# Two transformer-like blocks on one core: delta rule's products by chunk, masks for the SSM decays, a last block by halves, and first k-tiles one slab ahead

## The chip, the cores and the metric

The kernel is one program on one core of a Trainium2 chip. The metric is device time in microseconds (us) of one execution. PE is TensorE, PEld its weight loads, ACT ScalarE, DVE VectorE, POOL GpSimd, SP the queue engine that issues most DMAs.

## What is computed

All arrays are float32: 256 tokens, width 2048. The first block is a norm and a projection to an SSM (32 heads of 64, 4 groups, chunks of 128 tokens) and to windowed attention with sinks, their output projection, a gated feed-forward of width 5632 with a short convolution, and an embedding (`pe`) that is normalised and added through a gate:

```python
gate = jax.nn.sigmoid(_rmsnorm(h, ple_norm_g[i]) @ w_ple_gate[i])
pe = _rmsnorm(p[i] @ w_ple_proj[i], ple_post_g[i])
h = h + gate * pe
```

The second block has a gated delta rule in both directions (8 heads of 128, chunks of 64 tokens), a Fourier branch, gates, an output projection, an MLP of width 8192 with squared relu, and the last norm. Of the delta rule, each chunk needs the inverse of a unit lower triangular 64x64 matrix:

```python
kb = k * beta
m = jnp.where(strict, jnp.einsum("bhnid,bhnjd->bhnij", kb, k) * decay, 0.0)
a_mat = m + jnp.eye(CHUNK, dtype=m.dtype)
rhs = jnp.concatenate([v * beta, kb * jnp.exp(gc)[..., None]], axis=-1)
sol = lax.linalg.triangular_solve(a_mat, rhs, left_side=True, lower=True, unit_diagonal=True)
```

In the SSM, the decay between tokens s and l of a chunk is the exponential of the sum of `dt * a` over the tokens after s up to l.

## The kernel before, in words

**The weight stream.** All large weights come as 238 quads of 4 slabs. A slab is 128 x 1024 float32: two k-tiles by 512 columns. For each slab SP loads `w_raw` (after DVE's `lo_ready` of the slab in the same place), ACT casts it to `w_hi` (after PE's `slab_done` of the slab before in that place), DVE subtracts to get `w_lo`. PE then makes 12 matmuls of 512 columns: two k-tiles, two token tiles `t` of 128, and three products (high by high, high by low, low by high), as `slab` writes them, into the pair of banks `psum[t]`. A `chunk` is 8 slabs, a product of full depth 2048 by 512 columns. Each engine's order is written out by hand in its own block, and semaphores tie them. `split` is the name of the cast on ACT and of the subtraction on DVE.

**The activations** (`a_hi`, `a_lo`) are made per tile of two k-tiles: PE transposes four squares of h (`operand_tiles`, line 2078), ACT scales and rounds to `a_hi` (`gained`, line 752), DVE makes `a_lo` (`gained_rest`, line 1297). The first chunk of the program is `first_chunk`: it transposes four tiles, and then tile s+4 ahead of slab s.

**SSM groups.** In each of four groups and for both token tiles, PE makes rows of summed decays from `adt` broadcast and a triangle `before` (line 2216), DVE subtracts each head's own sum and clips at 0 (line 1522, eight instructions), ACT takes the exponential of `ssm_w`, POOL multiplies by the scores (line 611), and PE applies it (`within`, line 2228). POOL also roots, scales and rotates q and k in `qk_norm`, between these products. `qk_square` shares memory with `ssm_y`.

**End of the first feed-forward and the gates.** PE makes the embedding (line 2378), then the last down projection and with it the transposes for the gate product. DVE does `normalize(pe_tok, ...)` (line 1322) in one piece before it adds the down products to h (line 1361). The gate product is four chunks, each with a sigmoid and a multiplication by `pe_tok`.

**Delta rule.** Four turns, two heads each. A unit is a token tile by a direction, 128 x 128, with two chunks on its diagonal. The triangular inverse is made in levels 1 to 5 (level 0 by a mask): `level_z` (line 2469), ACT's copy to `zz` (line 1156), `level_rz` (line 2477), DVE's update (line 1827), transposes `turned` (line 2487) and DVE's copy. POOL masks for the next level (line 686) and makes scaled copies of q, k and v, the query's at level 1 (line 694). Half slabs of the gates' weight stream (`gate_slab`) stand between these products on PE. After the levels come `uw` (2564, 2565) and four steps of the state, whose products are 64 wide (`of_state` line 2502, `output_of_state` line 2495), and for which forward and backward direction write different halves of the partitions.

**The last block.** The MLP runs in 16 blocks of 512 hidden columns: an up chunk, transposes of `m_stage` (line 2146), relu (1243), square (1246) and gating (1993), `m_lo` (1999), then `mlp_down` of two quads. The last one is followed by the squares of h, the mean, POOL's root, the scaling and four output transfers (line 518).

## Time and profile before

| | |
|---|---|
| median of the runs | 3024.98 us (3024.2 to 3029.27, 3 runs) |
| the profiled execution | 3025.64 us, of which the span 3023.8 us |
| PE, PEld, DVE, ACT, POOL busy | 98%, 81%, 67%, 47%, 10% |
| DMA | 525.71 MB, mean 174 GB/s |
| mean granted clock of PE | 0.996 |

Times in the profile count from the span's start. Busy shares are of the span; a matmul's records overlap with the next one's, so the distance between starts, not their length, is what each costs. PEclk is the granted clock: 1.00 is 2.4 GHz, 0.50 is 1.2 GHz.

### The profile page before, as it was taken

Reading aid. Unit: us, or ns where it says so; the run is one execution under the profiler, and the core shown is the slowest. Engines: PE = TensorE matmul, PEld = TensorE weight load, DVE = VectorE, ACT = ScalarE, POOL = GpSimd, SP = SyncE. Lnnn points to the kernel's source line nnn. Section 1 sums busy time; section 2 is a strip of 40 time slices with the busy share of each in tenths; the row PEclk is TensorE's granted clock in tenths of the full one; section 3 lists DMA queues with packets and bytes.
Section 4 is the critical chain, followed back from the end, with each engine's and each line's share of the span. In section 5 each row is a group of like instructions: output and inputs, shape, how many; then the busy total and the mean of one; then the engine's idle time right before and its main releaser. Section 6 shows DMA issues by size and latency. Waiting matters only on the chain.

```text
span 3023.8 us, 42408 instructions
## 1 busy us (share of the span) xinstructions
PE 2973.5 (98%) x14487; PEld 2455.1 (81%) x14487; DVE 2015.8 (67%) x2667; ACT 1410.5 (47%) x1797; POOL 314.3 (10%) x275
## 2 busy tenths in 40 slices
PE   8999999999999999999999999999999999999997
PEld 7888777788888888886878888888888888888886
DVE  6765877656677776667577667776655666666665
ACT  6444446544444444445555543333545444444443
POOL 0003860000000000000000154333000000000000
PEclk9999999999999999999999999999999999999999
DMA  6554443466555555553565433332765565555554
GB/s 221 178 186 159 140 147 132 156 196 210 182 189 178 194 188 194 187 188 125 188 214 187 166 119 112 112 118 96 240 219 195 186 192 189 186 191 188 188 182 135
DMA packets 145653, 525.71 MB, mean 174 GB/s; under 512 B 16416, under 2 KB 17184, under 8 KB 144800
## 3 DMA queue, kind: packets, MB, share of 16 engines
q1 hardware_dynamic: 140416, 504.25, 51.0%
q0 software_dynamic: 1536, 11.78, 1.1%
q10 hardware_dynamic: 3616, 8.52, 0.9%
q8 instruction: 57, 0.93, 0.1%
q14 instruction: 28, 0.23, 0.0%
HBM read 516.09 MB, written 8.39 MB: 173 GB/s over the span
## 4 chain that ended last, share of the span: by engine, by line
PE 65%; issue 25%; DVE 4%; POOL 3%; ACT 1%; DMA 1%; DVEq 0%; ACTq 0%; POOLq 0%; SPq 0%
PE bank L2053 19%; PE bank L2055 19%; PE bank L2054 19%; DVE w_lo L1283 1%; PE bank L2146 1%; PE bank L2477 1%; PE bank L2469 1%; PE bank L2078 1%; ACT w_hi L727 1%; POOL qk_rs L563 1%; DMA w_raw<-weights 0%; PE bank L2284 0%; PE bank L2487 0%; POOL delta L694 0%; POOL delta L686 0%
## 5 line engine op out<-in xcount | busy, mean ns | idle before, releaser
L1283 DVE TENSOR_TENSOR w_lo<-w_raw,w_hi 128x1024 fp32r<-128x1024 f32 x952 | 1193.9, 1264 | 789.6 <-ACT w_hi L727 788.7
L727 ACT CAST w_hi<-w_raw 128x1024 fp32r<-128x1024 f32 x952 | 1000.0, 1052 | 1410.7 <-PE bank L2055 1386.7
L2053 PE MATMUL bank<-w_hi,a_hi 128*128 128x512 f32 x2816 | 1118.9, 397 | 2.1 <-DVE w_lo L1283 1.7
L2055 PE MATMUL bank<-w_hi,a_lo 128*128 128x512 f32 x2816 | 1098.6, 390 | 0.0
L2054 PE MATMUL bank<-w_lo,a_hi 128*128 128x512 f32 x2816 | 1097.6, 390 | 0.0
L2053 PEld LDWEIGHTS bank<-w_hi,a_hi 128*128 128x128 f32 x2816 | 529.8, 188 | 115.9 <-issue 9.5
L2055 PEld LDWEIGHTS bank<-w_hi,a_lo 128*128 128x128 f32 x2816 | 529.2, 188 | 112.2
L2054 PEld LDWEIGHTS bank<-w_lo,a_hi 128*128 128x128 f32 x2816 | 530.0, 188 | 106.3 <-issue 1.9
L539 POOL TENSOR_TENSOR rstd<-rstd,neg_half 128x2 f32<-128x2 f32 x7 | 5.5, 787 | 1927.1 <-DVE rstd L1312 1927.1
L2053 PE MATMUL bank<-w_hi,m_hi 128*128 128x512 f32 x512 | 200.1, 391 | 5.1 <-DVE m_lo L1999 5.1
L2055 PE MATMUL bank<-w_hi,m_lo 128*128 128x512 f32 x512 | 200.0, 391 | 0.0
L2054 PE MATMUL bank<-w_lo,m_hi 128*128 128x512 f32 x512 | 199.9, 390 | 0.0
L1361 DVE TENSOR_TENSOR h<-h,bank 128x512 f32<-128x512 f32 x240 | 153.6, 681 | 22.2 <-PE bank L2055 22.2
L2053 PE MATMUL bank<-w_hi,f_hi 128*128 128x512 f32 x352 | 139.8, 397 | 0.0
L2055 PE MATMUL bank<-w_hi,f_lo 128*128 128x512 f32 x352 | 138.1, 392 | 0.0
L2054 PE MATMUL bank<-w_lo,f_hi 128*128 128x512 f32 x352 | 137.9, 392 | 0.0
L2053 PEld LDWEIGHTS bank<-w_hi,m_hi 128*128 128x128 f32 x512 | 96.6, 189 | 25.5 <-DVE m_lo L1999 5.4
L2054 PEld LDWEIGHTS bank<-w_lo,m_hi 128*128 128x128 f32 x512 | 96.6, 189 | 20.1
L2055 PEld LDWEIGHTS bank<-w_hi,m_lo 128*128 128x128 f32 x512 | 96.5, 189 | 20.1
L2055 PEld LDWEIGHTS bank<-w_hi,f_lo 128*128 128x128 f32 x352 | 66.6, 189 | 14.1
L2054 PEld LDWEIGHTS bank<-w_lo,f_hi 128*128 128x128 f32 x352 | 66.7, 190 | 13.8 <-issue 0.2
L2053 PEld LDWEIGHTS bank<-w_hi,f_hi 128*128 128x128 f32 x352 | 66.7, 189 | 13.6 <-DVE f_lo L1669 0.2
(383 smaller groups left out, 2488.9 us busy)
## 6 DMA issues: line engine op xcount, KB each, us to landing
w_raw<-weights SPq DMA_DIRECT2D x952, 512.0 KB, 4.2
gate<-gate_st ACTq DMA_DIRECT2D x8, 512.0 KB, 3.3
h<-gate ACTq DMA_DIRECT2D x8, 512.0 KB, 5.2
gain<-gains POOLq DMA_DIRECT2D x3, 1024.0 KB, 7.2
h<-x_tok SPq DMA_DIRECT2D x4, 512.0 KB, 9.9
w_proj_sb<-w_proj POOLq DMA_DIRECT2D x1, 2048.0 KB, 10.0
h_rest<-h POOLq DMA_DIRECT2D x1, 2048.0 KB, 13.3
h<-h_rest POOLq DMA_DIRECT2D x1, 2048.0 KB, 10.1
```

The lines of the kernel that those rows point to most:

```text
L539: nc.gpsimd.tensor_tensor(rstd[:, n], rstd[:, n], neg_half[:, 0:TT], ALU.pow).then_inc(rstd_ready, 1)
L563: nc.gpsimd.tensor_tensor(rs, rs, neg_half[:, 0:TT * heads8].rearrange("p (t a) -> p t a", t=TT), ALU.pow).then_inc(qk_rstd, 1)
L727: nc.scalar.copy(w_hi[:, s, :], w_raw[:, s, :]).then_inc(hi_ready, 1)
L1283: V.tensor_tensor(w_lo[:, s, :], w_raw[:, s, :], w_hi[:, s, :].bitcast(F32), ALU.subtract).then_inc(lo_ready, 1)
L1361: V.tensor_tensor(h[:, t, col], h[:, t, col], pair[p][t][:], ALU.add).then_inc(pair_free[p], 1)
L2053: T.matmul(psum[t][:], left_hi[:, ts], wh, start=first, stop=False)
L2054: T.matmul(psum[t][:], left_hi[:, ts], wl, start=False, stop=False)
L2055: last = T.matmul(psum[t][:], left_lo[:, ts], wh, start=False, stop=final)
L2078: last = T.transpose(bank[4 + i % 4][:, k * SEQ + t * P:k * SEQ + (t + 1) * P], src[:, t, (2 * i + k) * P:(2 * i + k + 1) * P], ident[:])
L2146: last = T.transpose(bank[first + ct // 2][:, (ct % 2) * SEQ + t * P:(ct % 2) * SEQ + (t + 1) * P], src[:, t, col0 + ct * P:col0 + (ct + 1 ...
L2469: last = T.matmul(hd.at(2, n), hd.mk[:, t, d], hd.r[:, t, d], start=True, stop=True)
L2477: last = T.matmul(hd.at(2, n), hd.t[:, t, d], hd.zz[:, t, d], start=True, stop=True)
```

## The change

It has these parts.

1. `slab`: all products with the high part of the weights first (after `hi_ready`), then those with the low part (after `lo_ready`). The count is the same.
2. `first_chunk` and ACT's and DVE's beginning: two tiles are transposed first, then tile s+1 ahead of slab s; ACT and DVE make tile s+1 before they split slab s. SP loads in another order.
3. SSM decays: DVE writes `ssm_later`, a mask times `adt`, PE multiplies it by `before`, ACT takes the exponential from the banks. POOL's `qk_norm` becomes `qk_scaled` and `qk_rotated`, and the rotation of tile 0 comes after the second product with the scores. `qk_square(0)` moves to the memory of `bT`.
4. The embedding is scaled per chunk in the gates.
5. Delta rule: the scores and both products of each level are made by chunk (`by_chunk`: two products of 64 x 64 in place of one of 128 x 128); the query's scaling on POOL comes at level 5; slab 8 is halved, with one half ahead of `uw`; DVE's order of splits and updates shifts.
6. The last block: gating and `m_lo` by halves and before DVE's last split; the last two column chunks by token tile; sum, mean, root, scaling and output by token tile.

```diff
@@ sync
-            for c in range(DC):
+            def piece(c):
                 cols = slice(c * NC, (c + 1) * NC)
                 sp_.dma_start(h[:, :, cols], small["x_tok"][:, :, cols]).then_inc(piece_loaded[c], 16)
-                sp_.dma_start(w_raw[:, c, :], wstream[0, c]).then_inc(raw_loaded[c], 16)
+            def first_slab(s):
+                sp_.dma_start(w_raw[:, s, :], wstream[0, s]).then_inc(raw_loaded[s], 16)
+            piece(0)
+            first_slab(0)
+            first_slab(1)
+            piece(1)
+            first_slab(2)
+            first_slab(3)
+            piece(2)
+            piece(3)
@@ gpsimd, SSM group
                     if t == 0:
                         qk_root(g)
-                    qk_norm(g, t)
+                        qk_scaled(g, 0)
+                qk_rotated(g, 0)
+                qk_scaled(g, 1)
+                qk_rotated(g, 1)
@@ gpsimd, delta rule: in the loop over levels k
                             nc.gpsimd.tensor_tensor(hd.eT, hd.eT, cums, ALU.mult).then_inc(dn_eTm, 1)
-                            pool.wait_ge(dn_egb, hd.of(i))
-                            q_rows = hd.qk[:, 0].rearrange("p (t s) -> p t s", t=TT).unsqueeze(2).to_broadcast(shape)
-                            nc.gpsimd.tensor_tensor(hd.qd, hd.qd, q_rows, ALU.mult).then_inc(dn_qd, 1)
...
+                        else:
+                            pool.wait_ge(dn_egb, hd.of(i))
+                            q_rows = hd.qk[:, 0].rearrange("p (t s) -> p t s", t=TT).unsqueeze(2).to_broadcast(shape)
+                            nc.gpsimd.tensor_tensor(hd.qd, hd.qd, q_rows, ALU.mult).then_inc(dn_qd, 1)
@@ scalar, beginning (DVE's has the same order)
+            gained(TR_ATTN, C_ATTN, 0)
             for s in range(QUAD):
-                gained(TR_ATTN, C_ATTN, s)
+                gained(TR_ATTN, C_ATTN, s + 1)
                 split(0, s, s + 1, first=True)
-            for s in range(2):
-                gained(TR_ATTN, C_ATTN, QUAD + s)
+            for s in range(QUAD - 1):
+                gained(TR_ATTN, C_ATTN, QUAD + s + 1)
                 split(Q_XBC + 1, s, s + 1)
-            gained(TR_ATTN, C_ATTN, 6)
-            gained(TR_ATTN, C_ATTN, 7)
-            split(Q_XBC + 1, 2, QUAD)
+            split(Q_XBC + 1, QUAD - 1, QUAD)
@@ scalar, SSM group
                 def decays(t):
-                    act.wait_ge(seg_ready, TT * g + t + 1)
-                    nc.scalar.activation(ssm_w, ssm_w, ACT.Exp).then_inc(seg_exp, 1)
+                    n = TT * g + t
+                    act.wait_ge(row_mm, n + 1)
+                    if n:
+                        act.wait_ge(ydiag_mm, n)
+                    for b in range(2):
+                        last = nc.scalar.activation(ssm_w[:, 4 * b:4 * b + 4].rearrange("p a s -> p (a s)"), bank[4 + b][:], ACT.Exp)
+                    last.then_inc(seg_exp, 1)
@@ vector, SSM
+            def later_tokens(n):
+                g, t = divmod(n, TT)
+                shape = [P, HPG, P]
+                if n:
+                    dve.wait_ge(row_mm, n)
+                V.scalar_tensor_tensor(ssm_later, before[:].unsqueeze(1).to_broadcast(shape), 0.0,
+                                       adt[:, t, g * HPG:(g + 1) * HPG].unsqueeze(2).to_broadcast(shape), ALU.is_equal, ALU.mult).then_inc(seg_ready, 1)
@@ vector, end of the first feed-forward, and per chunk of the gates
-            normalize(pe_tok, pe_tok, N_POST, G_POST)
+            mean_square(N_POST)
...
+                normalized_piece(pe_tok, n, N_POST)
                 for t in range(TT):
                     dve.wait_ge(sig_ready, TT * n + t + 1)
+                    dve.wait_ge(normed, NORMED[G_POST - 1] + TT * n + t + 1)
@@ vector, the last block
+            j = N_FF2 - 1
+            for b in range(2):
+                half = slice(2 * b, 2 * b + 2)
+                dve.wait_ge(ff_silu, N_FF + 2 * j + b + 1)
+                V.tensor_tensor(m_act[:, half].rearrange("p k s -> p (k s)"), m_relu[:, half].rearrange("p k s -> p (k s)"),
+                                bank[6 + b][:], ALU.mult).then_inc(ff_mul, 1)
+                dve.wait_ge(ff_mul, N_FF + 2 * j + b + 1)
+                dve.wait_ge(ff_hi, N_FF + 2 * j + b + 1)
+                V.tensor_tensor(m_lo[:, half], m_act[:, half], m_hi[:, half].bitcast(F32), ALU.subtract).then_inc(ff_lo, 1)
+            mlp_down(N_QUADS - 4, range(D // NC - 1, D // NC))
@@ tensor, slab
+                pe.wait_ge(hi_ready, QUAD * q + s + 1)
+                for j in part:
+                    wh = w_hi[:, s, j * NC:(j + 1) * NC]
+                    for t in range(TT):
+                        for n, left in enumerate(products[j]):
+                            T.matmul(psum[t][:], left[:, t * P:(t + 1) * P], wh, start=start and j == 0 and n == 0, stop=False)
                 pe.wait_ge(lo_ready, QUAD * q + s + 1)
                 for j in part:
-                    left_hi, left_lo = products[j]
-                    wh = w_hi[:, s, j * NC:(j + 1) * NC]
                     wl = w_lo[:, s, j * NC:(j + 1) * NC]
                     for t in range(TT):
-                        ts = slice(t * P, (t + 1) * P)
-                        first = start and j == 0
-                        final = stop and j == SLAB_KT - 1
-                        T.matmul(psum[t][:], left_hi[:, ts], wh, start=first, stop=False)
-                        T.matmul(psum[t][:], left_hi[:, ts], wl, start=False, stop=False)
-                        last = T.matmul(psum[t][:], left_lo[:, ts], wh, start=False, stop=final)
+                        last = T.matmul(psum[t][:], products[j][0][:, t * P:(t + 1) * P], wl, start=False, stop=stop and j == SLAB_KT - 1)
@@ tensor, first_chunk
-                for i in range(4):
+                for i in range(2):
                     operand_tiles(n, src, ready, i)
                 def tiles_of(s):
-                    if s + 4 < KT // 2:
-                        operand_tiles(n, src, ready, s + 4)
+                    if 0 < s < KT // 2 - 1:
+                        operand_tiles(n, src, ready, s + 1)
                     pe.wait_ge(a_lo_ready, KT // 2 * n + s + 1)
@@ tensor, SSM group
-                        last = T.matmul(bank[4 + a // 4][:, (a % 4) * P:(a % 4 + 1) * P],
-                                        adt[:, t, g * HPG + a:g * HPG + a + 1].to_broadcast([P, P]), before[:], start=True, stop=True)
+                        last = T.matmul(bank[4 + a // 4][:, (a % 4) * P:(a % 4 + 1) * P], ssm_later[:, a], before[:], start=True, stop=True)
@@ tensor, delta rule
+                chunks = [slice(c * CHUNK, (c + 1) * CHUNK) for c in range(P // CHUNK)]
+                def by_chunk(out, left, right):
+                    for r in chunks:
+                        last = T.matmul(out[r, r], left[:, r], right[:, r], start=True, stop=True)
+                    return last
...
-                            last = T.matmul(hd.at(2, n), hd.mk[:, t, d], hd.r[:, t, d], start=True, stop=True)
+                            last = by_chunk(hd.at(2, n), hd.mk[:, t, d], hd.r[:, t, d])
...
-                            last = T.matmul(hd.at(2, n), hd.t[:, t, d], hd.zz[:, t, d], start=True, stop=True)
+                            last = by_chunk(hd.at(2, n), hd.t[:, t, d], hd.zz[:, t, d])
```

## Rows read from the trace of the kernel before

**Rows 1.** Who waited for whom, PE: total us, times, longest.

```profile
PE bank L2053 <- DVE m_lo L1999: 5.1, 1, 5.1
PE bank L2228 <- POOL work L611: 3.7, 4, 1.8
PE bank L2078 <- DVE h L1361: 3.5, 1, 3.5
...
PE bank L2469 <- POOL delta L686: 2.1, 4, 0.5
PE bank L2053 <- DVE w_lo L1283: 1.7, 1, 1.7
```

**Rows 2.** Windows: stretch, length, busy us of PE, PEld, DVE, ACT, POOL, PEclk.

```profile
1401.30:1408.10 6.80, 6.08 (x17) 4.82 (x18) 3.90 (x6) 3.11 (x7) 0.00 (x0) 0.50 0.59 177
322.60:326.10 3.50, 3.50 (x17) 3.31 (x16) 2.89 (x5) 0.00 (x0) 3.42 (x2) 0.51 0.78 267
```

**Rows 3.** Timeline, PE, its last matmuls: start us, length, instruction.

```profile
3010.83 0.39 PE L2053 MATMUL bank<-w_hi,m_hi 128*128 128x512 f32 x1
...
3011.28 0.39 PE L2055 MATMUL bank<-w_hi,m_lo 128*128 128x512 f32 x1
```

**Rows 4.** Groups of instructions, PE: one product of the levels; busy, mean ns.

```profile
L2477 PE MATMUL bank<-delta 128*128 128x128 f32 x320 | 39.1, 275 | 0.0
```

**Rows 5.** Timeline, PE: a block of one level, second turn.

```profile
1872.18 0.39 PE L2055 MATMUL bank<-w_hi,a_lo 128*128 128x512 f32 x1
1872.42 1.95 PE L2477 MATMUL bank<-delta 128*128 128x128 f32 x16
...
1874.43 0.40 PE L2054 MATMUL bank<-w_lo,a_hi 128*128 128x512 f32 x1
```

**Rows 6.** Timeline, PE: a block of the state, 64 wide.

```profile
1910.43 0.39 PE L2055 MATMUL bank<-w_hi,a_lo 128*128 128x512 f32 x1
1910.75 0.66 PE L2502 MATMUL bank<-delta 128*64 128x128 f32 x8
1911.23 0.61 PE L2495 MATMUL bank<-delta 128*64 128x128 f32 x8
...
1912.11 0.40 PE L2054 MATMUL bank<-w_lo,a_hi 128*128 128x512 f32 x1
```

**Rows 7.** Timeline, PE: an SSM block of 64 columns.

```profile
300.08 1.97 PE L2228 MATMUL bank<-work 128*128 128x64 f32 x16
```

**Rows 8.** Timeline: ACT and PE between level 5's products.

```profile
1891.97 0.59 ACT L1156 COPY delta<-bank 128x512 f32<-128x512 f32 x1 [0.71 <-PE bank L2469]
1892.66 2.00 PE L2477 MATMUL bank<-delta 128*128 128x128 f32 x16
```

**Rows 9.** Timeline: PE and ACT in the first chunk.

```profile
10.29 1.04 ACT L727 CAST w_hi<-w_raw 128x1024 fp32r<-128x1024 f32 x1 [1.54 <-DMA w_raw<-weights]
...
14.87 0.78 PE L2053 MATMUL bank<-w_hi,a_hi 128*128 128x512 f32 x1
...
25.96 0.60 PE L2078 MATMUL bank<-ident_sb,h 128*128 128x128 f32 x4
...
26.32 0.48 PE L2053 MATMUL bank<-w_hi,a_hi 128*128 128x512 f32 x1
26.60 0.84 ACT L752 ACTIVATE a_hi<-bank,gain_col_sb 128x256 fp32r<-128x256 f32 x2 [1.30 <-PE bank L2078]
...
27.33 1.05 ACT L727 CAST w_hi<-w_raw 128x1024 fp32r<-128x1024 f32 x1
```

**Rows 10.** Timeline, DVE: the embedding's scaling.

```profile
1394.24 5.39 DVE L1322 SCALAR_TENSOR_TENSOR pe_tok<-pe_tok,rstd,gain 128x512 f32<-128x512 f32 x8 [0.83 <-POOL rstd L539]
```

**Rows 11.** Timeline: the last block and the output.

```profile
2983.64 1.15 ACT L1246 ACTIVATE m_hi<-m_relu 128x512 fp32r<-128x512 f32 x2
...
2986.34 1.28 DVE L1999 TENSOR_TENSOR m_lo<-m_act,m_hi 128x512 fp32r<-128x512 f32 x2
...
3016.41 3.21 SPq L518 DMA_DIRECT2D out<-xn_m  x4
```

More of the change, by code:

```diff
@@ L1999, in mlp_gated, with mlp_down @@
                     V.tensor_tensor(m_lo[:, half], m_act[:, half], m_hi[:, half].bitcast(F32), ALU.subtract).then_inc(ff_lo, 1)
[L2001 to L2010 removed]
+            def mlp_down(q, chunks=range(D // NC)):
+                for n in chunks:
+                    split(q + 1 + n // 2, 2 * (n % 2), 2 * (n % 2) + 2)
                     dve.wait_ge(slab_done, QUAD * q + 2 * (n + 1))
@@ L2017, in _, with mlp_up @@
             mlp_evac(q, 0)
-            with dve.Fori(0, N_FF2 - 1) as j:
+            def mlp_up(j):
                 q = Q_MLP + 2 + 4 * j
@@ L2023, in _ @@
                 mlp_evac(q, 2)
-                mlp_down(q + 2, 2)
-            mlp_gated(N_FF2 - 1)
-            mlp_down(N_QUADS - 2, 1, last=True)
-            mean_square(N_OUT)
-            root_of(N_OUT)
+            with dve.Fori(0, N_FF2 - 2) as j:
+                mlp_up(j)
+                mlp_down(Q_MLP + 4 + 4 * j)
+            mlp_up(N_FF2 - 2)
+            mlp_down(N_QUADS - 4, range(D // NC - 1))
+            j = N_FF2 - 1
+            for b in range(2):
+                half = slice(2 * b, 2 * b + 2)
+                dve.wait_ge(ff_silu, N_FF + 2 * j + b + 1)
[4 more added lines that the diff above has]
+                V.tensor_tensor(m_lo[:, half], m_act[:, half], m_hi[:, half].bitcast(F32), ALU.subtract).then_inc(ff_lo, 1)
@@ new lines, in _ @@
+            dve.wait_ge(gain_loaded, 16 * (G_OUT + 1))
+            for n in range(2):
+                split(N_QUADS - 1, 2 * n, 2 * n + 2)
+                dve.wait_ge(slab_done, QUAD * (N_QUADS - 2) + 2 * (n + 1))
+                add_to_h(n, slice(n * NC, (n + 1) * NC))
+                for t in range(TT):
+                    out_gain(t, n)
+            for t in range(TT):
+                for n in range(2, DC):
+                    dve.wait_ge(slab_done, QUAD * (N_QUADS - 1 + t) + 2 * (n - 1))
+                    col = slice(n * NC, (n + 1) * NC)
+                    V.tensor_tensor(h[:, t, col], h[:, t, col], pair[n % 2][t][:], ALU.add).then_inc(pair_free[n % 2], 1)
+                    if n == 2:
+                        out_gain(t, n)
+                end_mean_square(t)
+                if t == 0:
+                    out_gain(t, DC - 1)
@@ L2540, in _ @@
                         for t in range(TT):
-                            ts = slice(t * P, (t + 1) * P)
-                            last = T.matmul(hd.at(1, TT * (1 - a) + t), hd.qk[:, 1, ts], hd.qk[:, a, ts], start=True, stop=True)
+                            for r in chunks:
+                                ts = slice(t * P + r.start, t * P + r.stop)
+                                last = T.matmul(hd.at(1, TT * (1 - a) + t)[r, r], hd.qk[:, 1, ts], hd.qk[:, a, ts], start=True, stop=True)
                     last.then_inc(dn_kk, 1)
@@ L2566, in _ @@
                     last.then_inc(dn_uw, 1)
-                for n in range(8, 11):
+                gate_slab(8, [1])
+                for n in range(9, 11):
                     gate_slab(n)
@@ L2664, in _ @@
                 mlp_block(j)
-            pe.wait_ge(ff_lo, N_FF + 2 * N_FF2)
-            mlp_down(N_QUADS - 2, U_MLP + 2 * (N_FF2 - 1))
+            use = U_MLP + 2 * (N_FF2 - 1)
+            for n in range(2):
+                pe.wait_ge(pair_free[n], 2 * (use + 2 - n))
+                for s in range(2):
+                    pe.wait_ge(ff_lo, N_FF + 2 * (N_FF2 - 1) + s + 1)
+                    slab(N_QUADS - 2, 2 * n + s, [(m_hi[:, 2 * s + k], m_lo[:, 2 * s + k]) for k in range(SLAB_KT)],
+                         pair[n], s == 0, s == 1)
+            for t in range(TT):
+                ts = slice(t * P, (t + 1) * P)
+                for n in range(2, DC):
+                    pe.wait_ge(pair_free[n % 2], 2 * (use + 3 - n % 2))
+                    for i in range(2 * n - QUAD, 2 * n - QUAD + 2):
+                        pe.wait_ge(lo_ready, QUAD * (N_QUADS - 1) + i + 1)
+                        for k in range(SLAB_KT):
+                            tile = 2 * (i % 2) + k
+                            wh, wl = (x[:, i, k * NC:(k + 1) * NC] for x in (w_hi, w_lo))
+                            T.matmul(pair[n % 2][t][:], m_hi[:, tile, ts], wh, start=tile == 0, stop=False)
+                            T.matmul(pair[n % 2][t][:], m_lo[:, tile, ts], wh, start=False, stop=False)
+                            last = T.matmul(pair[n % 2][t][:], m_hi[:, tile, ts], wl, start=False, stop=tile == 3)
+                        last.then_inc(slab_done, 1)
 def _slabs(w, k_major=False):
```

157 lines of the change are left out of this document (89 added, 68 removed).

## The prediction

> **What bounds the kernel now.** I read the page first: TensorE (PE) is busy 98% of the span (the table), and the matmuls of the weight stream follow each other without a hole: from the first of the two rows to the second are two steps in 0.45 us, 0.225 to 0.227 each, so a slab of 12 takes 2.72 us [rows 3]. So only two things are worth time: work that PE does, and the few places where it stands still. The list of PE's waits has the second [rows 1]: 5.1 us before the last MLP block (m_lo), 3.7 us in the SSM groups (work, from POOL), 3.5 us at the end of the first feed-forward (h, from DVE), 2.1 us in the delta rule (delta, from POOL), 1.7 us for one late w_lo. Two of these stops were followed by a stretch at the lower clock: the windows show 3.5 us at 0.51 and 6.8 us at 0.50, that is 1.2 instead of 2.4 GHz [rows 2].
>
> **Delta rule by chunk.** The products of the levels are 128x128 by 128 columns. The group of one of the two lines has 320 instructions [rows 4]; 5 levels, 8 products and 4 turns are 160, so each product is two instructions. Now each product becomes four: 64 wide, 64 columns. A block of 16 with a 128-wide stationary costs, from the last slab matmul before it to the second after it, 1874.43 - 1872.18 = 2.25 us [rows 5]. 16 instructions 64 wide, still 128 columns, cost 1912.11 - 1910.43 = 1.68 us [rows 6]: 8 lie in 0.61 us, one lasts 0.28 [rows 4], so 0.33 us hold the three steps of four pairs, 0.11 a pair, against 0.111 for a single one 128 wide (1.95 less 0.28, over 15, [rows 5]). Two halves of the array work side by side. The fixed part of such a block is 1.68 - 8 x 0.109 = 0.81 us, against 2.25 - 16 x 0.111 = 0.47: entering and leaving the narrow form costs 0.34. The new block has 16 pairs with half the columns, which no row shows. If the columns set the pair, it takes 0.055; if instructions do not start faster than in rows 6, 0.109. For the second speaks nothing but that it is the least seen; for the first, that a full-width instruction takes the same 0.11 with 128 columns, and that 64 columns did not help where the stationary stayed 128 wide (16 in 1.97 us, [rows 7]): there the load of 128 columns sets the pace, and here that load is halved too. I take 0.062, near the first. Block: 16 x 0.062 + 0.81 = 1.80, that is -0.45 us; ends -0.57 and +0.30. Per turn there are 8 such blocks in the levels and one of scores (kk): -4.05. The last level's two products are one block of 32: 32 x 0.062 + 0.81 = 2.79 against 4.02, -1.23; but between them stands ACT's copy, which even now ends at 1892.56 for a start at 1892.66 [rows 8]. With the first product of a head halved the second waits: two copies in a row, 1.18 us, and about 0.3 to reach each side; +0.7. So -4.6 a turn, -18.3 in four. The other levels keep half a slab between their products, 1.36 us, which covers a copy of 0.59. The query decay moves behind level 5, and POOL's 2.1 us [rows 1] go. Half a slab more between the products costs another entry, 0.24 x 4 = +1. Sum -19.4 (ends -25 and +11).
>
> The rows say that the change of form costs 0.34 us a block. The Trainium skill ("TensorEngine Tiling (Array Packing)", Tiling Modes) says that changing the tiling mode drains TensorE, which speaks against mixing narrow blocks with full-width slabs as here. It gives no figure; without any drain the new block would be 1.46 us and the delta rule would save 13 us more, and the measured row decides.
>
> **The start.** This one goes the other way. Before, ACT makes a_hi of tile s, then the cast of slab s, and PE transposes four tiles ahead: tile to slab 0.36 us [rows 9]. After, ACT makes a_hi of tile s+1 before the cast of slab s, and PE transposes tile s+1 only after slab s-1. So slab s can't start before transposes, ACT's a_hi and ACT's cast are through: 0.64 (25.96 to 26.60) + 0.84 + 1.05 + 0.05 = 2.58 us after the first transpose instead of 0.36 [rows 9], 2.2 us for each of the slabs 1 to 6: +13.3. ACT is in order, so the cast cannot pass; that the high part comes first does not help, since it is the high part that is late. On the credit side slab 0 starts when its cast ends, 11.3 instead of 14.87 [rows 9], 3.5 us earlier, but three tiles of 0.36 are then still to do: -2.5. After the cast of slab 6 ACT has one more (1.05), eight squares of h, each about the 0.6 of rows 11, and a narrow cast, which DVE has to split before PE's narrow product: 1.05 + 4.9 + 1.2 = 7.15, against 5.44 for PE's slabs 6 and 7: +1.7. Sum +12.5, ends +10 and +19; the long end is where the stops keep the clock low. I take +13.
>
> **SSM decays.** DVE's pass between PE's rows and ACT's exponential goes (ACT reads PSUM), and POOL multiplies before it rotates; DVE's mask is made a step ahead. The 3.7 us [rows 1] go, with half of the 3.5 us at the lower clock [rows 2]: -5.4 (ends -3 and -6). PE's work is the same count. Late next is the SSM norm, which DVE bounds; unchanged.
>
> **Embedding at the gates.** DVE's scaling, 5.39 us in one piece [rows 10], stood ahead of the add to h that PE waited for. It goes into the gate chunks of 22 us, 1.35 us each, eight slabs long, where DVE has a third of its time idle (the table): nothing. The 3.5 us go, and half of PE's 6.08 busy us at the lower clock [rows 2]: -6.5 (ends -5, -7).
>
> **High part first.** A slab waits for ACT's cast, no longer for DVE's 1.2 us. In the steady stream both are there: nothing. At the late weight (1.7 us, [rows 1]): -1.2 (0 to -2). The order of the matmuls keeps count and loads.
>
> **The end.** The last m_lo comes half by half, ahead of DVE's split and add. From the start of the squares, 2983.64, half a square (0.58) and half a lo (0.64) lead to about 2984.8 [rows 11] instead of PE's start 2.9 us later (5.1 us wait, [rows 1]). Then the output of the first token tile is scaled and sent while PE works on the second: after PE's end at 3011.7 [rows 3] the old tail is 12.1 us, four transfers of 512 KB from 3016.41 on [rows 11]; half of them go (-3.5), and the shorter row of adds, squares and scalings gives about as much as the new order behind ACT (a wait of 1.3) and one of 0.9 for pair 1 take: net -6.3 (ends -4, -8.5).
>
> **Sum.** +13 - 5.4 - 6.5 - 1.2 - 19.4 - 6.3 = -25.8 us on the profiled execution's 3025.64: 2999.8. The median of the runs is 0.7 lower: 2999.
>
> **Rivals.** 1: narrow instructions start no faster than in rows 6, the pair stays at 0.109. Every block costs 0.3 more; +10.6 instead of -19.4: 3029. The Trainium skill ("TensorE: Matmul & The Clock Gate") gives some 62 ns a matmul for the sequencer with hardware decode off; the 0.055 of rows 6 is already under that, so the trace disagrees. Chance 0.15.
> 2, the slower one: in each product the narrow instructions do not pair, since its two passes over one half follow each other, and each takes the 0.11 of rows 7. Then a product costs 0.44 instead of 0.22: 352 products, +77 and the entries: about 3100. It decides (slower by 0.2%) from a mean of 0.056 an instruction on. Rows 6 pair with the same order of halves, against it. Chance 0.03.
> 3: the start does not stall, because ACT's chain is hidden in some way that I miss; -2 instead of +13: 2984. Against it stand two engines in order. Chance 0.12.
> 4: the stops of 2.2 us at the start, or those left in the last block, keep the clock low as the stop in rows 2 did, so that three to five slabs more take twice their 2.72 us: about 3009. Chance 0.12.
> The forecast has 0.58; its own range is 2992 to 3005.
>
> **Numbers.** 2982 to 3022 takes in the forecast, rivals 3 and 4 and the middle of rival 1's pitches. 0.2%, 6 us, is what this kernel's measurement can tell: faster 0.81, same 0.12, slower 0.07.
>
> **What would show it.** Level blocks of 16 pairs near 1.8 us (right) or 2.5 (rival 1); PE waiting for ACT's w_hi six times near 2.2 us before 55 us; the first narrow product at 52 to 53 us instead of 40; no wait for POOL in the SSM and delta stages; the last block's first matmul about 2.5 us after its transposes; under 9.5 us from PE's last matmul to the end. Wrong it would be made by the pair's pace above all: 704 pairs, 0.7 us for each nanosecond.

## The result and the profile after

The changed kernel takes 3011.07 us (median of 5 runs, 3006.83 to 3012.19) against 3025.06 us before (median of 5, 3024.20 to 3029.27), that is 14 us faster where 26 were forecast. The ratio worked out from all runs is 0.9947, 95% interval 0.9935 to 0.9959; that of the two medians is 0.9954. The profiled execution spans 3009.0 us against 3023.8.

Both kernels run the same 952 slabs in the same order, so the start of each slab's first matmul on PE can be set side by side. This table is worked out from the two traces:

```
slab          before     after    after - before
0               14.9      11.5      -3.4
8               46.6      67.6     +21.0    end of the first chunk, narrow product done
120            406.7     422.3     +15.6    end of the SSM groups
126            429.6     446.8     +17.2    behind the SSM norm
452           1408.4    1419.1     +10.7    gates begun
504           1562.0    1571.8      +9.8    behind the late weight
625           2069.4    2059.2     -10.2    delta rule done
900           2860.0    2849.7     -10.3    MLP
last matmul   3011.3    2999.0     -12.3
end           3023.8    3009.0     -14.8
```

So the first chunk loses 21.0, and everything else together gains 35.8. Term by term, forecast against trace: start +13 (12.5 as worked out), +21.0; SSM -5.4, -5.4, of which 1.6 are lost again right behind it; embedding -6.5, -6.5; high part first -1.2, -0.9; delta rule -19.4, -20.0; the end -6.3, -4.5.

The list of PE's waits of the changed kernel, which answers to [rows 1] (line waited for: total us, times, longest):

```profile
PE bank L2137 <- ACT w_hi L754: 14.6, 7, 2.9
...
PE bank L2583 <- DVE delta L1882: 2.4, 4, 0.6
PE bank L2137 <- issue: 2.3, 1, 2.3
PE bank L2137 <- ACT gate_st L1169: 1.5, 4, 0.4
PE bank L2554 <- ACT delta L1190: 1.5, 7, 0.2
```

The first line is new and the largest: ACT's cast in the first chunk, seven times. The waits for POOL's `work` (3.7 before, 0.9 now, once), for h (3.5) and for m_lo (5.1) are gone or down to 1.1 and 2.3, and three small ones stand in the delta rule in place of POOL's 2.1.

One slab of the first chunk, timeline of PE, ACT and DVE, answering to [rows 9]:

```profile
23.52 0.60 PE L2165 MATMUL bank<-ident_sb,h 128*128 128x128 f32 x4
24.16 0.84 ACT L779 ACTIVATE a_hi<-bank,gain_col_sb 128x256 fp32r<-128x256 f32 x2 [5.20 <-PE bank L2165]
24.89 1.04 ACT L754 CAST w_hi<-w_raw 128x1024 fp32r<-128x1024 f32 x1
...
26.07 0.47 PE L2137 MATMUL bank<-w_hi,a_hi 128*128 128x512 f32 x1 [1.96 <-ACT w_hi L754]
...
26.39 0.51 PE L2137 MATMUL bank<-w_hi,a_lo 128*128 128x512 f32 x1
...
26.70 0.63 PE L2137 MATMUL bank<-w_hi,a_hi 128*128 128x512 f32 x1
...
27.12 0.63 PE L2137 MATMUL bank<-w_hi,a_lo 128*128 128x512 f32 x1
```

From the start of the transposes to the slab's first matmul are 2.55 us (26.07 - 23.52), against 0.36 before: 2.19 a slab, as forecast. What was not in the forecast stands in the last lines: the matmuls start 0.42 us apart, not 0.227. 512 columns in 0.427 us is the 1.2 GHz level. The windows of the whole stretch and of the one behind it (columns as in [rows 2]):

```profile
19.00:54.20 35.20, 25.32 (x81) 19.36 (x82) 10.85 (x16) 9.25 (x16) 0.00 (x0) 0.76 0.28 92
54.20:68.00 13.80, 11.97 (x76) 9.83 (x76) 9.81 (x21) 13.16 (x28) 1.25 (x1) 1.00 0.41 126
```

The granted clock is 0.76 over slabs 1 to 5 and 1.00 once the slabs follow each other again. It is not low throughout: it falls in each of these five slabs, for 6 to 8 matmuls, and is up again before the slab ends. Some 44 distances between matmuls of this chunk are of 0.427 us, and 8 of before's. 9 and 8 of these lie in slab 0, ahead of the first record of the clock in either trace.

A block of the levels, PE, answering to [rows 5]:

```profile
1873.98 0.62 PE L2142 MATMUL bank<-w_lo,a_hi 128*128 128x512 f32 x2
1874.53 1.15 PE L2554 MATMUL bank<-delta 128*64 128x64 f32 x32
1875.62 0.50 PE L2137 MATMUL bank<-w_hi,a_hi 128*128 128x512 f32 x1
1875.95 0.39 PE L2137 MATMUL bank<-w_hi,a_lo 128*128 128x512 f32 x1
```

The last slab matmul ahead starts at 1873.98 + 0.62 - 0.39 = 1874.21, so the block costs 1875.95 - 1874.21 = 1.74 us (forecast 1.80, before 2.25). One instruction lasts 0.22, so 31 steps take 0.93: 0.030 an instruction, 0.060 a pair. Of the block, 16 x 0.060 = 0.96 is that, and the fixed part 0.78.

### The profile page after: what moved, and what is told of

It reads as the page before. It is cut to its first block, busy times and chain, and to the rows that moved or that the text cites. A ratio compares the mean times of both kernels' runs of the same rounds, so it can differ in the third digit from the quotient of the medians.

```text
span 3009.0 us, 43769 instructions
## 1 busy us (share of the span) xinstructions
PE 2955.5 (98%) x15191; PEld 2422.7 (81%) x15191; DVE 2010.2 (67%) x2615; ACT 1411.7 (47%) x1807; POOL 322.5 (11%) x276
## 4 chain that ended last, share of the span: by engine, by line
PE 91%; DVE 3%; issue 2%; ACT 2%; POOL 1%; DMA 1%; DVEq 0%; ACTq 0%; POOLq 0%; SPq 0%
PE bank L2137 55%; PE bank L2142 27%; PE bank L2234 1%; DVE w_lo L1341 1%; ACT w_hi L754 1%; PE bank L2554 1%; PE bank L2165 1%; DMA w_raw<-weights 1%; PE bank L2583 0%; PE bank L2372 0%; PE bank L2305 0%; PE bank L2466 0%; PE bank L2316 0%; PE bank L2242 0%; DVE delta L1875 0%
## 5 line engine op out<-in xcount | busy, mean ns | idle before, releaser
L2137 PE MATMUL bank<-w_hi,a_hi 128*128 128x512 f32 x2816 | 1125.5, 400 | 16.5 <-ACT w_hi L754 14.6
L2142 PE MATMUL bank<-w_lo,a_hi 128*128 128x512 f32 x2816 | 761.4, 391 | 0.0
L2137 PE MATMUL bank<-w_hi,m_hi 128*128 128x512 f32 x496 | 193.5, 390 | 2.3 <-issue 2.3
L2137 PE MATMUL bank<-w_hi,m_lo 128*128 128x512 f32 x496 | 193.4, 390 | 0.0
L2142 PE MATMUL bank<-w_lo,m_hi 128*128 128x512 f32 x496 | 133.5, 391 | 0.0
L2137 PEld LDWEIGHTS bank<-w_hi,m_lo 128*128 128x128 f32 x496 | 93.4, 188 | 19.4
L2142 PE MATMUL bank<-w_lo,f_hi 128*128 128x512 f32 x352 | 94.2, 389 | 0.0
```

What stands on the lines that cost most here:

```text
L2137: T.matmul(psum[t][:], left[:, t * P:(t + 1) * P], wh, start=start and j == 0 and n == 0, stop=False)
L2142: last = T.matmul(psum[t][:], products[j][0][:, t * P:(t + 1) * P], wl, start=False, stop=stop and j == SLAB_KT - 1)
```

## The experiments

**1. Everything but the start.** The changed kernel with the old beginning on SP, ACT, DVE and PE (part 2 of the change undone).

```diff
@@ tensor, first_chunk
-                for i in range(2):
+                for i in range(4):
                     operand_tiles(n, src, ready, i)
...
-                    if 0 < s < KT // 2 - 1:
-                        operand_tiles(n, src, ready, s + 1)
+                    if s + 4 < KT // 2:
+                        operand_tiles(n, src, ready, s + 4)
@@ scalar, vector, sync: the old order too
```

> The changed kernel with the old beginning (four tiles transposed ahead, ACT's and DVE's old order, SP's old loads). Theory: the start alone costs 20.9 us in the changed kernel (slab 8 starts at 67.6 instead of 46.7), and nothing later gives it back, so about 2990 us, 0.9885 of before. Rival, that the start only moves time which a later stage would have waited for anyway (a DMA or POOL's work that is due at a fixed time): more than 2995 us, with new waits behind slab 8.

Measured: 2989.39 us, as expected; ratio 0.9882 (0.9867 to 0.9898). Slab 8 starts 21.1 us earlier than in the changed kernel and the last matmul 21.6 earlier. Nothing behind takes it back: the weight stream and POOL were not waiting for a fixed moment.

**2. The start alone.** The kernel before with part 2 only.

> The kernel before with only the new beginning (SP's, ACT's, DVE's and PE's order in the first chunk); a slab still waits for DVE's low part before its first product. Theory: the same stops and clock, and the wait for the low part on top (1.2 us for each of seven slabs, where the low part is not hidden behind eight products): 3046 us plus up to 8, so 3046 to 3055. Rival, that the order of the products in a slab does not matter here: 3046 us at most.

Measured: 3054.24 us, 1.0099 (1.0083 to 1.0114), upper end of what was expected. Slab 60 starts 23.9 us late and not 21.0. PE's waits for DVE's w_lo in the whole run, and for POOL:

```profile
PE bank L2061 <- DVE w_lo L1292: 24.0, 8, 4.1
...
PE bank L2237 <- POOL work L621: 6.3, 4, 3.3
```

Of the 24.0 us, 23.4 in seven waits lie in the first chunk, against 14.6 in seven in the changed kernel: 3.21 us ahead of each of slabs 1 to 6 and not 1.95. So in a first chunk of this form, the high part first does help. The stop stays, but DVE's 1.2 us a slab lie behind it instead of in it. Slab 8 is all the same only 3.0 us later than in the changed kernel, because the clock, which the expectation took to be the same, was not. The windows of slabs 1 to 3 and of slabs 4 and 5:

```profile
19.00:39.00 20.00, 10.30 (x48) 8.03 (x48) 6.36 (x10) 5.37 (x10) 0.00 (x0) 1.00 0.33 112
39.00:54.00 15.00, 10.06 (x27) 7.87 (x28) 3.62 (x5) 2.09 (x4) 0.00 (x0) 0.66 0.20 70
```

Slabs 1 to 3 run at the upper level behind stops of 3.21 us each, longer than those of the changed kernel; then slab 4 and most of slab 5 run at the lower one. So a stop in every slab does not by itself bring the clock down in every slab.

The further 4 us between slabs 60 and 120 belong to the second line, to which the last section comes back.

**3. ACT's and DVE's order alone.** The changed kernel, two pairs of lines turned on ACT, and the same on DVE; PE's order and SP's loads stay.

```diff
             for s in range(QUAD):
-                gained(TR_ATTN, C_ATTN, s + 1)
                 split(0, s, s + 1, first=True)
+                gained(TR_ATTN, C_ATTN, s + 1)
             for s in range(QUAD - 1):
-                gained(TR_ATTN, C_ATTN, QUAD + s + 1)
                 split(Q_XBC + 1, s, s + 1)
+                gained(TR_ATTN, C_ATTN, QUAD + s + 1)
```

> The changed kernel, only ACT's and DVE's order in the first chunk turned: the weight slab s is cast and split before tile s+1 is scaled. PE's order and SP's loads stay as changed. Theory: PE's stops come from ACT's order alone, so they go, the clock stays at its upper level from about 19 us on, slab 8 starts near 43 us (11.5 + 8 x 2.72 + the transposes), and the time is 2986 us. Rival, that PE's transposing one slab ahead is itself too late (a_hi of tile s+1 not there when slab s ends): stops of 1 us or more stay, above 2995 us.

Measured: 2990.82 us, 0.9889 (0.9874 to 0.9904). The stops are gone: slabs 1 to 6 start 3.2 us apart, 2.72 and the transposes. So PE's transposing one slab ahead is no loss; what stopped PE is that ACT's cast of slab s stood behind the scaling of a tile that PE had only just transposed (the list names ACT's w_hi; DVE's turn was not run by itself). The time is 4 to 5 us above the expectation. The largest waits that are left, next to one for a DMA at the very start:

```profile
...
PE bank L2137 <- ACT w_hi L754: 2.8, 1, 2.8
PE bank L2165 <- DVE a_lo L1347: 2.6, 1, 2.6
PE bank L2213 <- DVE w_lo L1469: 2.5, 1, 2.5
```

The first stands ahead of slab 0 and the second at the SSM norm, in the changed kernel as here. The last one is the narrow product's low part, behind ACT's eight squares: slab 7 starts at 36.0, slab 8 not before 48.0, that is 12.0 us where the kernel before takes 9.3. Of the 5 us that slab 8 is late against the expected 43, this is 2.7; for the rest the expectation had counted too little between slabs 7 and 8.

**4. The stops filled.** The changed kernel; behind the transposes of tiles 2 to 7, PE gets eight more products into a bank that nobody reads. They are work on top and change no result.

```diff
                     if 0 < s < KT // 2 - 1:
                         operand_tiles(n, src, ready, s + 1)
+                        for _ in range(8):
+                            T.matmul(bank[2][:], a_hi[:, 0, 0:P], a_hi[:, 0:2].rearrange("p k s -> p (k s)"), start=True, stop=True)
```

> The changed kernel with eight extra 512-column products into an unused bank behind the transposes of each of tiles 2 to 7, that is 8 x 0.227 = 1.8 us of work in the stop of about 2 us; they change no result. ACT's order, and so the stop, stays. Theory: of the 20.9 us, 8 are the lower clock that follows idling; with PE at work in the stops the clock comes up and the slabs take 2.72 instead of 4.4 us, so 3001 to 3004 us in spite of more work. Rival, that the lower clock at the start has nothing to do with PE standing still: the extra products take 8 x 0.427 = 3.4 us, longer than the stop, and the time is 3018 us or more.

Measured: 3001.08 us, 0.9921 (0.9907 to 0.9934): 48 more matmuls of 512 columns, and 10 us less. The timeline and the windows:

```profile
27.30 0.60 PE L2165 MATMUL bank<-ident_sb,h 128*128 128x128 f32 x4
27.66 2.10 PE L2186 MATMUL bank<-a_hi 128*128 128x512 f32 x8
...
29.86 0.47 PE L2137 MATMUL bank<-w_hi,a_hi 128*128 128x512 f32 x1
30.16 0.40 PE L2137 MATMUL bank<-w_hi,a_lo 128*128 128x512 f32 x1
30.40 0.40 PE L2137 MATMUL bank<-w_hi,a_hi 128*128 128x512 f32 x1
```

```profile
19.00:46.00 27.00, 26.39 (x120) 20.34 (x121) 10.57 (x16) 9.01 (x16) 0.00 (x0) 1.00 0.35 121
```

The chain over ACT is as long as before (2.56 from transposes to slab), but the clock is 1.00 and the slab's matmuls are 0.23 apart. Slab 8 starts 8.0 us earlier than in the changed kernel, so 21.0 splits into 13.0 for the stops, with the earlier slab 0 and the later narrow product, and 8.0 for the clock behind them. The first was forecast at 12.5. The other 2 us of the median are not the start's; they come from stretches at the lower clock further on, of which this profile has fewer.

**5. By chunk alone.** The kernel before with `by_chunk` in `level_z`, `level_rz` and the scores, nothing else.

```diff
-                            last = T.matmul(hd.at(2, n), hd.mk[:, t, d], hd.r[:, t, d], start=True, stop=True)
+                            last = by_chunk(hd.at(2, n), hd.mk[:, t, d], hd.r[:, t, d])
...
-                            last = T.matmul(hd.at(2, n), hd.t[:, t, d], hd.zz[:, t, d], start=True, stop=True)
+                            last = by_chunk(hd.at(2, n), hd.t[:, t, d], hd.zz[:, t, d])
```

> The kernel before with the scores and both products of the levels by chunk, nothing else of the delta rule changed: the query's decay stays at level 1 on POOL, no slab is halved, DVE keeps its order. Theory: each of 32 blocks of 16 and four last levels saves what the changed kernel's rows show, 2.25 - 1.75 = 0.5 us a block, so -16 for the blocks, -5 for the kk blocks and last levels, and some of it is eaten by waits for POOL that grow when PE is early (2.1 us before, 5 expected): 3025 - 17 = 3008. Rival, that the saving is PE's alone and the chain over DVE's updates and POOL's masks sets the level: waits grow by as much as the blocks shrink, 3018 us or more.

**6. The whole delta rule part.** By chunk, the query's decay at level 5, slab 8 halved, DVE's order; the rest as before.

> The kernel before with the whole delta-rule part (by chunk, query's decay at level 5, slab 8 halved, DVE's order). Theory: the part gives in the old kernel what it gave in the changed one, 20 us (the slabs' lead grows from 9.7 to -10.3 us between slabs 540 and 625): 3005 us, 3 us under by chunk alone. Rival, that the moves around the products do nothing or harm: the same as by chunk alone, or above.

Measured together: 3012.78 us (3007.20 to 3016.24), 0.9954 (0.9941 to 0.9968) for by chunk alone, between the expectation and its rival; 3004.70, 0.9934 (0.9920 to 0.9947) for the whole part, as expected. Between slabs 540 and 625 the first gains 13.0 us, the second 19.8, as much as in the changed kernel (20.0). The waits of the first within that stretch:

```profile
PE bank L2466 <- POOL delta L686: 4.2, 8, 0.5
PE bank L2495 <- DVE delta L1827: 3.4, 4, 0.9
PE bank L2573 <- DVE delta L1827: 2.4, 4, 0.7
```

PE is through earlier, and POOL's masks and DVE's updates are not: 10.0 us of waits against 2.1 in these places before. Moving POOL's decay of the query out of level 1, half a slab ahead of `uw`, and DVE's order give 6.8 us more; which of the three gives how much was not run. The narrow products and the moves around them are one change: without the moves, a third of the 20 us is lost.

**7. The SSM part alone.**

> The kernel before with the SSM part alone. Theory: the four waits for POOL (3.7 us) and the 3.5 us at the lower clock go, -5.4 by slab 120 as in the changed kernel, and the 1.6 us that the changed kernel loses again at 443 us (a stretch at the lower clock behind the norm's wait) belong to where the stops fall, not to this part: 3019.5 to 3021 us. Rival, that the wait only moves to the norm: 3023 us or more.

Measured: 3020.28 us (11 runs, 3019.29 to 3022.52), 0.9981 (0.9972 to 0.9990). Slab 120 starts 5.4 us early, slab 126 3.8: the 1.6 us go here too, without any other part of the change, by the clock (last section); the expectation had put them down to the other parts. The wait for POOL does not move to the norm; its 2.6 us there are as before.

**8. The embedding, the last block and the high part first.** Three parts in three places, the rest as before.

> The kernel before with three parts that lie in different places of the span: the embedding scaled at the gates, the last block by halves and by token tile, the high part first. Theory: -6.5 at the end of the first feed-forward, -1 at the late weight, -4.5 in the last block, as the changed kernel's slabs show, so 3013 us. The trace shows each by itself. Rival for the last block, that its 2.3 us stop with 1.4 us of lower clock behind it is made by the parts before: more than 6 us saved behind slab 944.

Measured: 3017.89 us (11 runs, 3012.48 to 3020.97), 0.9971 (0.9962 to 0.9980), 5 us over the expected 3013. The profiled execution took 3013.80 and is the second shortest; what the longer ones lose has no trace. By its slabs: -6.5 at slab 452 (embedding), -0.8 at 504 (high part first), 1.6 lost again before slab 540 (a stretch at the lower clock at 1555 us), and behind slab 943 another 6.1, not 4.5. The rival's number for the last block came. The 2.3 us stop is there, so the parts before do not make it; what differs is the clock behind it. First the changed kernel, then this one:

```profile
2974.00:2981.00 7.00, 6.50 (x22) 5.20 (x23) 5.89 (x8) 1.77 (x3) 0.00 (x0) 0.76 0.40 111
```

```profile
2968.00:2990.00 22.00, 19.74 (x91) 16.23 (x91) 15.22 (x19) 10.53 (x15) 0.00 (x0) 1.00 0.36 120
```

**9 to 12. Towards a faster version.** The first takes experiment 3 and lays ACT's eight squares between the casts:

```diff
+                if s == QUAD - 1:
+                    first_squares(0)
                 gained(TR_ATTN, C_ATTN, s + 1)
...
                 split(Q_XBC + 1, s, s + 1)
+                first_squares(s + 1)
                 gained(TR_ATTN, C_ATTN, QUAD + s + 1)
             split(Q_XBC + 1, QUAD - 1, QUAD)
-            for c in range(DC):
-                act.wait_ge(piece_loaded[c], 16)
-                squares(h, xs, c)
```

> The changed kernel with ACT and DVE splitting slab s before tile s+1, as in the run before, and ACT's eight squares of h placed two at a time between the casts of slabs 3 to 6 instead of in one row behind slab 7's cast. Theory: what is left of the start is the wait of 2.5 us at 45 us for the narrow product's low part, because eight squares (5 us) stand ahead of its cast; between the casts they lie in ACT's idle time (2 of 3.2 us a slab are used), so slab 8 starts at 45.5 to 46 us instead of 48.0 and the time is 2988.5 us. Rival, that 3.1 us of ACT work a slab leave too little room and PE waits for w_hi instead: 2990.8 us or more.

The second is that and, in the delta rule, another order on DVE:

```diff
-                split(q + 1, 2, 4)
+                split(q + 1, 2, 3)
                 updates(2)
-                masked_scores()
-                split(q + 2, 0, 1)
+                split(q + 1, 3, 4)
                 updates(3)
-                split(q + 2, 1, 2)
+                split(q + 2, 0, 1)
                 updates(4)
-                split(q + 2, 2, 3)
+                split(q + 2, 1, 2)
                 updates(5)
-                split(q + 2, 3, 4)
+                masked_scores()
+                split(q + 2, 2, 4)
```

> The run beside it (squares between the casts) and in the delta rule DVE's order: one split between the updates of the levels instead of two ahead of the second, the masked scores behind level 5. Theory: PE's wait before the transposes of level 2 (0.6 us, four times, for DVE's update, which stands behind two splits) goes: 2.4 us less, 2986 us. Rival, that DVE is full over a level (its splits take up to 2.3 us here instead of 1.25) and the update of level 3 comes later in its place: a new wait of 0.5 us or more four times, no gain or a loss.

The third is the first with eight extra products at the stop ahead of the last block, the fourth is the second with them:

```diff
+            for _ in range(8):
+                T.matmul(bank[4][:], a_hi[:, 0, 0:P], a_hi[:, 0:2].rearrange("p k s -> p (k s)"), start=True, stop=True)
             use = U_MLP + 2 * (N_FF2 - 1)
```

> The run beside it (squares between the casts) and eight extra 512-column products into an unused bank at the stop of 2.3 us ahead of the last MLP block's down products. Theory: the lower clock after that stop, 8 slab matmuls at 0.427 instead of 0.227 us in the changed kernel, comes from PE standing still; with the stop filled it does not fall and 1.6 us come back: 2987 us. Rival, that such a stretch belongs to the moment and not to the stop: it stays, here or within 20 us of it, and the time is that of the run beside it.

> The run with DVE's new order plus the eight extra products at the last stop. Its partner does show the stretch at the lower clock behind that stop (seven slab matmuls 0.427 apart), which the run without DVE's order did not. Theory: with the stop filled the stretch is gone, 1.4 us less, 2982.5 us, the fastest of all. Rival, that the stretch is a matter of the moment: it is there in spite of the filling, or another one comes up elsewhere, and the time is 2984 us.

Measured: 2986.33 us (0.9872, 0.9855 to 0.9888) with the squares between, 2983.89 (0.9860, 0.9844 to 0.9877) with DVE's order too, 2986.88 (0.9873, 0.9857 to 0.9890) and 2984.09 (0.9857, 0.9841 to 0.9874) with the last stop filled. The squares bring slab 8 from 48.0 to 44.3, 45.3, 45.3 and 44.4 in the four profiles, a little earlier than the 45.5 to 46 expected; the 1 us between them is the lower clock of slab 0, which lasts longer in two. DVE's order takes the wait of 2.4 us for its update away and no other grows there; between slabs 540 and 625 PE gains 4.0. Of these, 2.4 and 2.8 us arrive in the medians: in both profiles with this order PE waits 3.2 us for ACT's `s_act` ahead of slab 504 (2.6 and 1.9 without it), for a reason that no run shows. The filling of the last stop is inconclusive by the times: with and without it, both pairs are equal. In the traces, the second run of the four has a stretch of 7 matmuls at 0.427 behind that stop and its filled partner has none (1.2 us less between slabs 900 and 945), but the first has none either, unfilled. The two versions of 2984 us are the fastest, 1.4% under the kernel before.

## Why the prediction came out as it did

The direction, and all terms but two, came out as worked out. The sum was 12 us too low, 8 of them by the clock at the start, 1.8 by the end and 1.6 behind the SSM norm. 3011 lies inside the stated range but outside the forecast's own, 2992 to 3005.

**The start: the term that failed.** "2.2 us for each of the slabs 1 to 6: +13.3", with the sum +12.5, is right for the stops (13.0 by experiment 4). What failed is that the term +13 puts the clock at next to nothing, and the chance of 0.12 given to rival 4: the stops keep the clock low. The prediction charged it to three to five slabs at twice their time and came to 3009; it was slabs 1 to 5 and 1.6 us each (4.42 us a slab instead of the 2.81 of slab 6, behind the same stop at the upper level), 8.0 in all by experiment 4, and the time 3011. That rival's number is near in part by luck: the clock fell anew in each slab and was up again before its end, instead of staying low. No reason against it was ever written, though single stops in rows 2 had brought the clock down. Experiment 2 shows that it was no certainty either: there slabs 1 to 3 kept the upper level behind longer stops. The range held the time because its upper end took this rival in.

"That the high part comes first does not help, since it is the high part that is late" was wrong. It does not end the stops, but without it each is longer: 23.4 against 14.6 us of waits (experiment 2).

The narrow product came at 60.96, not at 52 to 53, by the 8 us of clock; its own term, +1.7 behind slab 7, was +1.6 (from +19.4 at slab 6 to +21.0 at slab 8).

**Delta rule: right in sum, by parts that cancel.** The block was 1.74 for 1.80, since the pair took 0.060 for an assumed 0.062; rival 1 (0.109) and rival 2 are out. POOL's 2.1 us went as forecast. But three waits that the working did not have came up, 2.4 for DVE's update ahead of level 2's transposes, 1.5 for the gate's copy behind level 5, 1.5 for ACT's `zz`; of these only the last was seen (as +0.7 a turn). The form change cost what rows 6 gave: the fixed part is 0.78 against 0.81. The timeline at level 5 shows the last two, answering to [rows 8]:

```profile
1891.51 1.15 PE L2554 MATMUL bank<-delta 128*64 128x64 f32 x32
1892.24 1.07 ACT L1190 COPY delta<-bank 128x512 f32<-128x512 f32 x2 [0.44 <-PE bank L2554]
...
1892.88 1.17 PE L2554 MATMUL bank<-delta 128*64 128x64 f32 x32 [0.22 <-ACT delta L1190]
1893.20 1.09 ACT L1169 COPY gate_st<-bank 128x512 f32<-128x512 f32 x2
...
1894.44 0.49 PE L2137 MATMUL bank<-w_hi,a_hi 128*128 128x512 f32 x1 [0.38 <-ACT gate_st L1169]
```

PE waits 0.22 for the first head's copy only, since the second head's products follow in time; then its next slab needs a bank that ACT empties behind those copies. Per turn the level-5 wait was 0.2 and not 0.7.

**SSM and embedding: right in place and size.** Slab 120 is 5.4 us nearer than slab 60, slab 452 6.5 nearer than slab 420. That 1.6 us of the first are lost behind slab 123 was not foreseen: a stretch at the lower clock that before did not have.

**High part first** in the stream: -0.9 for a forecast of -1.2, at the late weight.

**The end: a term that was too large.** -6.3 was forecast, 2.9 from PE's earlier start and 3.5 from the output, with the new waits about paid for by shorter work. The changed kernel gives -4.5: 2.9 from the start, 2.5 behind PE's last matmul, less 0.9 that PE waits for pair 1, which nothing pays for. Kernel before and changed kernel both have the lower clock behind the stop. In experiment 8 it stays up, and the -6.1 there holds some 1.6 us of clock that the forecast had not counted, so it is near -6.3 by luck. The stop of 2.3 us was forecast (about 2.5 from the transposes to the first matmul; 2974.50 - 2972.24 = 2.26). After PE's end, 2999.0 + 0.4, come 9.6 us, a little over the 9.5 of the sign.

## What to carry to other kernels

When an order on one engine is changed so that it waits for fresh input of another, put the work that is already due ahead of the wait: turning two lines on ACT and on DVE gave back 20 us (experiment 3). A stop of PE that returns in every slab costs its own length and can cost the lower clock of the work behind it, here 13.0 + 8.0; price both, and where the stop can't go, filling it with idle products can still pay. When a product on PE is made cheaper, look at once at what DVE, ACT and POOL must deliver between two such products: here a third of the gain hung on moving their work.

## What the runs showed of the hardware

**Short stretches at the lower clock come and go with the same instructions.** Most last 6 to 10 slab matmuls 0.427 apart and cost 1.2 to 2 us each. Behind the SSM norm, PE stands still for 2.6 us in both kernels. The windows of before and of the changed kernel around this stop and the slab that follows:

```profile
423.00:430.00 7.00, 4.40 (x27) 3.60 (x25) 6.72 (x9) 2.59 (x4) 6.76 (x9) 1.00 0.32 84
```

```profile
440.00:448.00 8.00, 6.34 (x25) 5.19 (x26) 5.52 (x9) 2.10 (x4) 7.62 (x17) 0.79 0.39 131
```

Instructions and waits around it are alike, the clock is not. The same holds behind the stop of the last block (0.76 in the changed kernel, 1.00 in experiments 8 and 9) and at 1743 us, where no stop stands ahead, only 24 matmuls with 8 or 16 columns; there it cost 0.3 us net, since PE before waited 1.2 us for DVE a little later. So a single stop does not decide it; what does stays open. The profiles of all these kernels have between one and four of them behind the first chunk; a difference of 2 or 3 us between two kernels can be that alone. Stops in every slab do not settle it either: in the first chunk of the changed kernel the clock fell in slabs 1 to 5, in that of experiment 2, with longer stops, in slabs 4 and 5 only.

**Two products 64 columns wide run side by side.** A product of the levels by chunk has a stationary of 128 partitions x 64 columns and 64 moving columns: its output is 64 x 64, but it is still 128 deep. In the mean one starts every 0.030 us; by the single records of the trace the two of a pair start 0.007 us apart and the next pair 0.058 later. That is about half of the 0.11 of a single full-width product with 128 columns [rows 5]; the change into and out of the narrow form, 0.3 of the block's fixed 0.78 us, stays. The Trainium skill ("TensorE: Matmul & The Clock Gate", "Wait — 56ns, not 53.3ns?") gives some 62 ns a matmul for the sequencer with hardware decode off; by the trace an instruction starts every 30, so that bound is not at work here, and the trace says no more about it than this.

**POOL's small operations wait for DVE's subtraction, and with them the SSM groups.** The profiles of experiments 2, 5 and 6 lose 5.3 us between slabs 99 and 103, in code that is the same as before. POOL's scaling and rotation there, in the kernel before and in experiment 5:

```profile
327.62 1.05 POOL L571 TENSOR_TENSOR qkv<-qkv,qk_rs 128x512 f32<-128x512 f32 x1
328.74 1.62 POOL L573 TENSOR_TENSOR qkv<-qkv,row_sb 128x512 f32<-128x512 f32 x1
330.44 1.19 POOL L580 TENSOR_TENSOR xs<-qkv,cos 128x64 f32<-128x64 f32 x1
...
331.86 0.32 POOL L580 TENSOR_TENSOR xs<-qkv,cos 128x64 f32<-128x64 f32 x1
```

```profile
328.04 1.45 POOL L571 TENSOR_TENSOR qkv<-qkv,qk_rs 128x512 f32<-128x512 f32 x1
329.56 2.15 POOL L573 TENSOR_TENSOR qkv<-qkv,row_sb 128x512 f32<-128x512 f32 x1
331.80 0.33 POOL L580 TENSOR_TENSOR xs<-qkv,cos 128x64 f32<-128x64 f32 x1
...
332.36 1.30 POOL L580 TENSOR_TENSOR xs<-qkv,cos 128x64 f32<-128x64 f32 x1
```

Some are longer and some shorter; in all, POOL takes 1.0 us more in experiment 5. What decides is DVE's subtraction for `w_lo` (line 1283). Of the 96 operations of 128x64 in the SSM groups of these two profiles, the 15 that start while it runs are the only ones over 1.1 us, and each ends 0.18 us after it; 67 others take 0.31 to 0.33, and the 14 between (0.65 to 0.77) lie under other work of DVE. So a shift of a few hundredths of a microsecond between the two engines can decide: the rotation at 373.44 us in the kernel before starts 0.02 us ahead of the subtraction and takes 0.32, the same one in experiment 5, 0.03 us behind its start, takes 1.38. In these stretches the kernel before has the lower clock on PE at 323 us and the other three do not, so PE comes earlier by 1.1 us and DVE's subtractions lie elsewhere. PE's waits for `work` add up to 6.3 us instead of 3.7 (the longest 3.3 instead of 1.8), and a stretch at the lower clock follows. That the order of causes is this one was not tested by a run. That the kernel before has runs at 3024 and at 3029 fits it and was not tested either; with the SSM part alone eleven runs lie within 3.2 us. If so, the SSM part gives some of its gain as steadiness, which a single profile of before doesn't show.
